# A hybrid attention trunk: tiles of a mixer written out step by step, in another order on three engines, and row maxima negated by the reduction itself

## The reference, cut to what matters

```python
u = rmsnorm(h, mix_norm[l]);  z = u @ w_in[l]
(a_q, a_k, a_v, b_q, b_k, b_v, b_f, c_q, c_k, c_v, g) = split(z)
o_a = diff_attention(...)       # 4 heads: softmax(q1 k1) - lam * softmax(q2 k2), then @ v, RMSNorm
o_b = forgetting_attention(...) # 8 heads: softmax(q k + decay), then @ v
o_c = stick_breaking(...)       # 8 heads: log_sigmoid(-z), sums over later keys, exp, then @ v
m = sum_i sigmoid(gate_i) * (o_i @ proj_i);  h = h + m @ w_out[l]
```

## Time and profile before

| | us |
|---|---|
| median of three runs | 2625.9 |
| lowest and highest | 2625.86 and 2626.07 |
| the profiled execution, its own time | 2626.04 |
| its span, first to last instruction | 2624.2 |
| TensorE busy | 2572.3 |
| VectorE busy | 1453.4 |
| ScalarE busy | 1125.0 |

### The profile page before, as it was taken

One profiled execution on the slowest core, in us unless ns is written; L12 is line 12 of the kernel. 1 busy time (PEld: TensorE's weight loads), 2 busy tenths in 40 slices (PEclk: granted clock), 3 DMA queues, 4 the chain that ended last, 5 costly groups with the idle time before them and its releaser, 6 DMA issues.

```text
span 2624.2 us, 37098 instructions
## 1 busy us (share of the span) xinstructions
PE 2572.3 (98%) x11838; PEld 2123.8 (81%) x11838; DVE 1453.4 (55%) x2292; ACT 1125.0 (43%) x1888; POOL 3.5 (0%) x12
## 2 busy tenths in 40 slices
PE   7999999999999999999999999999999999999998
PEld 6888888777888888888888888888877888888886
DVE  5444347888854464444344443588887445544434
ACT  4222237777732242222232222478776223422222
POOL 0000000000000000000000000000000000000000
PEclk9999999999999999999999999999999999999999
DMA  4222331111122232223332223212111222322233
GB/s 165 96 96 96 105 103 65 57 57 57 57 89 97 96 113 96 96 97 103 104 105 96 97 95 112 88 57 65 57 57 57 96 96 91 119 96 96 96 105 103
DMA packets 65769, 238.07 MB, mean 91 GB/s; under 512 B 7296, under 2 KB 7552, under 8 KB 65408
## 3 DMA queue, kind: packets, MB, share of 16 engines
q1 hardware_dynamic: 65664, 236.79, 27.2%
HBM read 234.66 MB, written 2.10 MB: 90 GB/s over the span
## 4 chain that ended last, share of the span: by engine, by line
PE 87%; DVE 6%; issue 3%; ACT 3%; DVEq 0%; DMA 0%; ACTq 0%; SPq 0%
PE ps L372 28%; PE ps L374 27%; PE ps L373 27%; PE ps L513 2%; ACT area L758 2%; DVE stat L1194 2%; DVE area L1058 1%; DVE w_lo L1058 1%; DVE o_whole L1274 0%; ACT scratch L851 0%; PE ps L488 0%; PE ps L489 0%; PE ps L500 0%; PE ps L502 0%; DVE stat L1196 0%
## 5 line engine op out<-in xcount | busy, mean ns | idle before, releaser
L758 ACT ACTIVATE w_hi<-w_raw 128x1024 fp32r<-128x1024 f32 x441 | 468.3, 1062 | 1160.6 <-PE ps L374 1159.6
L372 PE MATMUL ps<-u_hi,w_hi 128*128 128x512 f32 x2368 | 931.0, 393 | 11.7 <-DVE w_lo L1058 11.3
L374 PE MATMUL ps<-u_hi,w_lo 128*128 128x512 f32 x2368 | 924.0, 390 | 0.0
L373 PE MATMUL ps<-u_lo,w_hi 128*128 128x512 f32 x2368 | 923.9, 390 | 0.0
L1058 DVE TENSOR_TENSOR w_lo<-w_raw,w_hi 128x1024 fp32r<-128x1024 f32 x441 | 538.7, 1222 | 314.2 <-ACT w_hi L758 306.9
L372 PEld LDWEIGHTS ps<-u_hi,w_hi 128*128 128x128 f32 x2368 | 445.8, 188 | 107.6 <-issue 16.9
L374 PEld LDWEIGHTS ps<-u_hi,w_lo 128*128 128x128 f32 x2368 | 445.5, 188 | 93.7
L373 PEld LDWEIGHTS ps<-u_lo,w_hi 128*128 128x128 f32 x2368 | 445.8, 188 | 90.6 <-issue 1.2
L372 PE MATMUL ps<-area,w_hi 128*128 128x512 f32 x1024 | 399.0, 390 | 0.4 <-DVE h L1078 0.4
L374 PE MATMUL ps<-area,w_lo 128*128 128x512 f32 x1024 | 398.6, 389 | 0.0
L373 PE MATMUL ps<-area,w_hi 128*128 128x512 f32 x1024 | 398.6, 389 | 0.0
(11 more groups left out here) (119 smaller groups left out, 1598.3 us busy)
## 6 DMA issues: line engine op xcount, KB each, us to landing
w_raw<-weights SPq DMA_DIRECT2D x441, 512.0 KB, 3.3
h<-x SPq DMA_DIRECT2D x2, 1024.0 KB, 6.7
out<-scratch SPq DMA_DIRECT2D x8, 256.0 KB, 2.2
scratch<-const_b SPq DMA_DIRECT2D x1, 512.0 KB, 10.5
scratch<-const_r SPq DMA_DIRECT2D x1, 320.0 KB, 9.7
scratch<-lambdas SPq DMA_DIRECT2D x1, 256.0 KB, 10.7
cst<-const SPq DMA_DIRECT2D x1, 137.0 KB, 2.3
par<-params SPq DMA_DIRECT2D x1, 94.0 KB, 2.0
```

The source lines that it names most:

```text
L372: pe.matmul(dst, hi, x_hi, start=start, stop=False, **kw)
L373: pe.matmul(dst, hi, x_lo, start=False, stop=False, **kw)
L374: return pe.matmul(dst, lo, x_hi, start=False, stop=stop, **kw)
L758: return act.activation(dst, src, ACT.Copy)
```

## The change

- The helpers that did four row blocks at once now do one; the programs of VectorE and ScalarE are written as lists of single steps, and steps of different helpers stand between one another. VectorE takes the four maxima of a head one after the other, ahead of the scalings, where before it took them in turn.
- `block_max` writes the negative maximum by the reduction itself (`negate=True`), with no multiplication behind it. 128 small multiplications are gone, and the column of `stat` between the two.
- On VectorE `take` and `split` come apart, and several steps change places: `turned_lo` stands ahead of `values_lo` at the start of a boundary, `rows` ahead of `output_whole(0)` at the end of a tile, `split(2)` between the last two scalings of the softmax before the boundary, `output_whole(1)` ahead of the maxima.
- On ScalarE `split(0)` stands between two steps of `softplus_hi`, `split(1)` between two of `stick_hi`, `split(2)` between the exponentials, `output_hi(2, t)` ahead of `exps(0, .)`, and `output_hi(1, t - 1)` between two exponentials.
- On TensorE attention work moves against the units by one to three blocks. The waits move into the functions that need them, with the same numbers.

TensorE at the boundary and in the tile:

```diff
             def rest_of_tile(unit):
-                pe.wait_ge(staged, c.next(staged, 2))
-                unit(0, 0, 3)
+                unit(0, 0, 6)
                 turn_values(0)
-                unit(0, 3)
+                unit(0, 6, 7)
                 turn_probs(1)
+                unit(0, 7)
                 unit(1, 0, 2)
                 weighted(1, 1)
                 scores(0, 0)
                 unit(1, 2, 7)
                 scores(0, 1)
                 unit(1, 7)
...
-                unit(5, 0, 3)
+                unit(5, 0, 4)
                 weighted(2, 0)
                 stick_scores(1)
-                unit(5, 3)
+                unit(5, 4)
...
                 scores(1, 0)
+                unit(7, 4, 5)
                 turn_values(1)
-                unit(7, 4)
-                unit(8, 0, 2)
+                unit(7, 5)
+                unit(8, 0, 1)
                 turn_probs(0)
-                unit(8, 2)
+                unit(8, 1)
                 weighted(1, 0)
                 scores(1, 1)
```

VectorE, the maximum, the end of a tile and the boundary (shortened: four like steps in a row stand on one line):

```diff
             def block_max(buf, i):
                 dve.wait_ge(score_set, c.next(score_set))
-                top = stat[:, 24 + i:25 + i]
-                dve.reduce_max(top, ps[:, SB0 + i, 0:(i + 1) * P], AX_X).then_inc(vec_done, 1)
-                dve.wait_ge(vec_done, c.next(vec_done))
-                dve.tensor_scalar(neg_max(buf, i), top, -1.0, None, ALU.mult).then_inc(max_set, 1)
+                dve.reduce_max(neg_max(buf, i), ps[:, SB0 + i, 0:(i + 1) * P], AX_X, negate=True).then_inc(max_set, 1)
...
                 take(8, 1.0)
+                block_max(1, 0)
+                block_max(1, 1)
+                block_max(1, 2)
                 qk_lo(0, 2, 7)
+                block_max(1, 3)
+                share_out(1, 0, prob_set)
+                share_out(1, 1, prob_set)
+                share_out(1, 2, prob_set)
                 split(2)
-                softmax(1, prob_set)
+                share_out(1, 3, prob_set)
+                rows(t + N_FOX, 0, 0)
+                rows(t + N_FOX, 0, 1)
                 output_whole(0)
-                for hd in range(2):
-                    rows(t + N_FOX, 0, hd)
...
-            def rest_of_tile(t, layer, project):
-                values_lo(0)
-                turned_lo()
-                stage(0, SCALE)
-                softmax(0, vec_done)
-                output_whole(1)
-                output_lo(1, t - 1, layer)
-                difference(layer)
-                stage(1, 1.0)
+            def rest_of_tile(t, layer, next_unit):
+                turned_lo(0) ... turned_lo(3)
+                next_unit(0, SCALE)
+                split(0)
+                values_lo(0)
+                block_max(0, 0) ... block_max(0, 3)
+                output_whole(1)
+                share_out(0, 0, vec_done) ... share_out(0, 3, vec_done)
+                block_max(1, 0) ... block_max(1, 3)
+                difference(0, layer) ... difference(2, layer)
+                next_unit(1, 1.0)
+                difference(3, layer)
+                output_lo(1, t - 1, layer)
+                split(1)
```

`stage` is `take` and then `split`; `share_out` is the scaling of one row block with its reciprocal; `next_unit` is `take` between tiles, and behind the last tile a wait alone. ScalarE at the boundary:

```diff
                 values_hi(0)
-                turned_hi()
+                turned_hi(0) ... turned_hi(3)
                 split(0)
                 output_rest(1)
-                exps(0)
-                output_hi(1, t - 1)
-                exps(1)
+                exps(0, 0) ... exps(0, 3)
+                exps(1, 0)
+                exps(1, 1)
+                output_hi(1, t - 1)
+                exps(1, 2)
+                exps(1, 3)
                 split(1)
```

More of the change, by code:

```diff
@@ L479, in weighted_whole, with weighted @@
                 last.then_inc(o_mm, 1)
-            def weighted(branch, hd):
+            def weighted(branch, hd, before=True):
+                if hd == 0:
+                    pe.wait_ge(v_set, c.next(v_set))
+                if (branch, hd) != (2, 0):
+                    pe.wait_ge(o_whole_set, c.next(o_whole_set))
+                elif before:
+                    pe.wait_ge(o_norm, c.next(o_norm))
                 for j in range(NQ):
@@ L520, in diff_norm, with unit @@
                 pe.matmul(ps[:, bank, :], ones, tile(7), start=True, stop=True).then_inc(o_ms, 1)
-            def unit(k, first_block=0, end=UNIT, first=False):
+            def unit(k, first_block=0, end=UNIT, first=False, before=True):
+                if first_block == 0 and (k > 1 or k == 0 and before):
+                    pe.wait_ge(staged, c.next(staged, 1 if k else 2))
                 last = u_unit(k % 2, k % SLOTS, (first_block, end), first)
@@ L552, in heads @@
                     rest_of_tile(unit)
-                    pe.wait_ge(staged, c.next(staged))
                     unit(2)
                     turn_probs(0)
+                    unit(3, 0, 3)
+                    weighted_whole()
+                    unit(3, 3, 5)
+                    diff_norm()
                 else:
-                    unit(0, first=True)
+                    unit(0, first=True, before=False)
                     sum_of_squares()
@@ L560, in heads @@
                     unit(1)
-                    pe.wait_ge(staged, c.next(staged))
                     unit(2)
[L563 to L571, removed]
+                    unit(3, 0, 5)
                     pe.wait_ge(pads_set, c.next(pads_set, 4))
@@ L829, in key_bias, with qk_hi @@
                         hi(k_bias(branch, hd)[half(1 - hd), :], tile(6)[half(1 - hd), :])
[L831 to L836, removed]
+            def qk_hi(branch, which, k, takes=1):
+                act.wait_ge(staged, c.next(staged, takes))
                 for hd in range(2):
@@ L940, in heads @@
                     rest_of_tile(t, project=True)
+                    qk_hi(2, 0, 0, 2)
+                    turned_hi(0)
+                    turned_hi(1)
+                    turned_hi(2)
+                    turned_hi(3)
                     qk_hi(2, 2, 1)
-                else:
-                    split_qk(2, 2, 1)
+                    output_square()
+                    split(2)
+                    output_rstd()
+                else:
+                    split(1)
+                    qk_hi(2, 2, 1)
@@ L944, in heads @@
                     key_bias()
[L945 to L952, removed]
+                    split(2)
+                stick_logs(0)
+                stick_logs(1)
+                stick_logs(2)
+                stick_logs(3)
+                stick_logs(4)
+                stick_logs(5)
+                softplus_hi(0)
@@ L1249, in values_lo, with stick_lo @@
+            def stick_lo(j):
+                dve.wait_ge(pt_hi_set, c.next(pt_hi_set))
+                lo(keys(PT_LO, j), key_block(0, j), keys(PT_HI, j)).then_inc(pt_set, 1)
             def values_lo(branch):
@@ L1301, in heads @@
             def heads(t, layer, before):
                 if before:
-                    rest_of_tile(t, layer, project=True)
-                    qk_lo(2, 0, 0)
-                    qk_lo(2, 2, 1)
-                else:
-                    qk_lo(2, 2, 1)
-                stage(2, 1.0)
-                stick_softplus()
+                    rest_of_tile(t, layer, take)
+                    turned_lo(0)
+                    turned_lo(1)
+                    turned_lo(2)
+                    turned_lo(3)
@@ L1310, in heads @@
+                    qk_lo(2, 0, 0)
+                qk_lo(2, 2, 1)
+                take(2, 1.0)
+                split(2)
+                stick_softplus(0)
+                stick_softplus(1)
+                stick_softplus(2)
+                stick_softplus(3)
+                softplus_lo(0)
+                softplus_lo(1)
+                softplus_lo(2)
+                softplus_lo(3)
                 if before:
                     output_lo(0, t - 1, layer)
-                stage(3, SCALE)
+                take(3, SCALE)
@@ L1313, in heads @@
                 values_lo(2)
[L1314 to L1325 removed]
+                stick_lo(0)
+                stick_lo(1)
+                stick_lo(2)
@@ new lines, in heads @@
+                stick_lo(3)
+                take(4, 1.0)
+                split(0)
+                split(1)
+                output_whole(0)
+                qk_lo(1, 0, 3)
+                stick_softplus(0)
+                stick_softplus(1)
+                stick_softplus(2)
+                stick_softplus(3)
+                softplus_lo(0)
+                softplus_lo(1)
+                softplus_lo(2)
+                take(5, 1.0)
+                softplus_lo(3)
+                rows(t * 2, 1, 0)
@@ new lines, in heads @@
+                qk_lo(1, 2, 4)
+                split(2)
+                stick_lo(0)
+                stick_lo(1)
+                stick_lo(2)
+                stick_lo(3)
+                take(6, SCALE)
+                split(0)
+                output_whole(1)
+                block_max(0, 0)
+                block_max(0, 1)
+                block_max(0, 2)
+                block_max(0, 3)
```

(26 more changed lines are left out.)

283 lines of the change are left out of this document (149 added, 134 removed).

## The result

| | before | after |
|---|---|---|
| median, us | 2625.88 | 2586.36 |
| lowest and highest | 2623.86 to 2626.07 | 2585.08 to 2586.66 |
| the profiled execution, its own time | 2626.04 | 2585.08 |
| its span | 2624.2 | 2583.3 |

Both medians are of four executions. The ratio of the times is 0.985, with a 95% interval of 0.9833 to 0.9867. Predicted were 2591 and 2587 to 2605. The direction and the mechanism came out as forecast; the gain is 39.5 us where 34.9 were forecast, and the range misses it by 0.6.

What follows compares the result with a forecast made beforehand. TensorE, busy for 98% of the span, was taken as the bound, losing time only in stalls at eight boundaries. 24.6 plus 10.2 plus 1.2 for the clock, less 0.4 and 0.8, gave 34.8 and 2591 us, range 2587 to 2605.

Steps and rivals of the forecast that it cites:

- (b): `weighted(1, 1)` at an inner boundary, waiting for `turned_lo`: 0.93 us lost before, ready with a margin of 0.6 after.
- the clock: Layer 2, behind the last boundary's stall: clock at 0.50 for 2.80 us, expected at 1.00 after, 1.2 us gained.
- 4.1 us: Sum of TensorE's five losses at an inner boundary, all expected to go, counted six times as 24.6.
- 5.1: TensorE's losses at the last boundary of a layer, with less matmul work as cover, counted twice as 10.2.
- less 0.4 and 0.8: Deductions: `weighted_whole` at the last boundaries (0.2, twice), and 0.8 for two added switches between kinds of matmul per tile.
- (a): `turn_probs(1)` at an inner boundary, waiting for the last row block of probabilities: 0.91 us lost before, margin 0.5 after.
- (c): `scores(0, 1)` at an inner boundary, waiting for the last exponential of the head ahead: 0.47 us lost before.
- (d): `turn_probs(0)` of the differential head at an inner boundary: 1.14 us lost before, last scaling 1.7 before its use after.
- (e): `weighted_whole` at a boundary: 0.65 us lost before, `turned_lo(0)` ready 0.7 before use at an inner boundary after.
- B: Rival: part of the stalls stays, VectorE 1.0 later loses 0.3 to 0.5 at four places per boundary: 2605, chance 0.21.
- C: Rival: the order brings nothing, only the negations do, at most 2.15 us a boundary: 2609, chance 0.05.
- S: Rival, slower: VectorE's new order makes it the bound of the tile through added idle waits: 2640, chance 0.04.

Runs made afterwards that it cites:

- The moved `values_lo`: The kernel before with one step moved, `values_lo(0)` behind `turned_lo` at the start of a boundary: 2626.18 us, ratio 1.0.
- The delays: The kernel after with extra VectorE instructions per tile: two ahead of `split(2)` 2590.47 us, four there 2595.79 us, two ahead of `take(1)` 2588.13 us.
- the order alone: The kernel after with the multiplication by -1 put back behind each maximum, the order staying new: 2597.66 us, ratio to before 0.9891.
- the negation alone: The kernel before with the maxima negated by the reduction, the order staying old: 2605.62 us, ratio to before 0.9923.

## Why the prediction was right, and where it failed

**The bound.** Right: TensorE alone sets the time, at the same rate as before, and the whole gain lies in the two mixers. From the first matmul of the mixer's unit 0 to the first product of its tail, layer 1 went from 350.62 to 331.54 us and layer 2 from 352.10 to 331.52, together 39.7. The two profiled executions differ by 1.3 us more, 0.9 of it in the sum of squares at the very end, whose two matmuls ran at a granted clock of 0.50 before (1.01 us from start to start) and at 1.00 after (0.53).

**The walk through the programs.** Right in its times: the last scaling was to end 0.5 before its use and ended 0.36 before; (b) 0.6 and 0.5; a tile of 77.3 and 76.92; two short waits at `weighted_whole`; 20 us less busy time on VectorE and 24 measured; the clock at 1.00 in layer 2.

**The step that failed is the size of the sum**: "4.1 us" for an inner boundary, "5.1" for a last one, and "less 0.4 and 0.8". The measured terms of an inner boundary, from segments of the two traces (each is good to 0.02):

| | counted | measured |
|---|---|---|
| unit 0, `take(8)` late | 0 | 0.19 |
| (a) | 0.91 | 0.91 |
| (b), and the slow second matmul behind it | 0.93 | 1.06 |
| (c) | 0.47 | 0.46 |
| (d), mean of the three | 1.14 | 1.16 |
| (e), and the slow second matmul | 0.65 | 0.84 |
| pieces of units | -0.1 | 0 |
| sum | 4.0 | 4.62 |

Taken as wholes, the six inner boundaries gave 27.9 instead of 24.0. The last boundaries gave 5.2 and 6.6, 11.8 with the clock, instead of some 10.8. Three mistakes are in it. I knew of the slow second matmul (1.6 us over the kernel) and put it in the range rather than in the sum. I priced the switches between kinds of matmul at 0.8 without a row of a switch that was new; the stretch from `diff_norm` to the second scores of branch 1, which holds the moved pieces, takes 46.64 us before and 46.63 after. And I looked for losses only where the view of waits had a line, and so put unit 0 at nothing (1.4 over eight boundaries). Together these are 3.8 of the 4.9 us by which the sum is short. Of the rest, (e) was taken from a mean over both kinds of boundary and is 0.07 too small at each inner one, and the clock gave back some 1.4 (6.6 less 5.2) where I took 1.2. The low end, "2587, where none of the losses is left", took over the same low sum; with the table's it would have been 2586.

**The stalls as terms.** Adding them up was right only because all of them closed; one is left, 0.33 us in front of `weighted_whole` at each last boundary. The moved `values_lo` shows that a stall eased alone can give nothing. The prediction gave the reason, VectorE busy for 28.01 of 31.93 us, and did not draw the conclusion.

**The rivals.** B did not happen. The delays show that one lateness is not paid four times; margins that fail at several places, each for a cause of its own, would still have added up. C was taken as unlikely and is refuted by the order alone, which brings 28.5 us. Its price for the negations alone, 2609, was near the 2605.62 of that kernel, but its "at most" was not a bound: 20.5 us came back where it had 17, since (d) at the last boundaries gave 1.2 and more and unit 0 was not in it. S did not happen: VectorE stands idle for 12.5 of the 76.92 us of an inner tile, and TensorE waits for none of it. `output_whole(1)`, which S had ahead of the maxima, stands behind the four maxima of the first head (541.94 in the trace after) and ahead of that head's scalings. The 0.36 at (a), of which 0.25 can be used up, is all the room there is at that place.

**DRAIN.** The prediction took from the Trainium skill (VectorE: DVE Perf Modes, "The DRAIN you can't avoid") that the next operation does not start before the pipe is empty, and found the trace against it. That was half of what is written there: the same section of the Trainium skill adds that a next operation that is not held starts earlier. With that the trace after agrees, with four maxima in 1.67 us instead of 1.94. The section of the Trainium skill also has a semaphore between two operations cost nothing extra. Here it costs about 0.1 us: the bound instruction starts 0.04 after the one ahead has ended, the unbound ones 0.05 to 0.08 before.

If a negation saved its 0.15 alone, that would be 3 x 4 x 0.15 = 1.8 us a boundary and 14 over eight. The kernel with the negation alone gained 20.5, and 19.1 without the 1.4 at unit 0, which is nearer to the 20.2 by the 0.21 of the earlier trace rows.

## What to carry to other kernels

When one engine sets the time and waits for another at several places in a row, find out whether these are several losses or one lateness paid in instalments: move one step, and see if the wait comes back at the next place. An added delay tells the same from the other side, and how much room there is. Then what counts is the start and the length of the late engine's chain, and an instruction of 0.15 us on it can be worth 0.2 us each time it runs. Take losses from the distances between starts, not from the view of waits, which leaves out whatever does not empty the pipe.

## What the runs showed of the hardware

A matmul whose semaphore comes just at its due time makes the matmul behind it late as well. In each of these traces all eight boundaries agree. With the VectorE instruction that gives the signal ending 0.04 us ahead of the due time, both were late, 0.32 and 0.33 from start to start against 0.23 in a stream. With 0.13 the first was on time and the second came 0.32 after it. With 0.52 (the negation alone, and TensorE's order of before with the other two programs of after) and with 1.2 (the kernel after) the distances are 0.23 and 0.24. So for these matmuls the end of the producer has to lie more than 0.13 us ahead, and 0.52 is enough; where between the two the loss ends was not measured. For the transposes 0.24 is enough: at the last boundary of the kernel after the scaling ends that far ahead of the transpose that reads it, and the ten still take 1.01 us.
